# Grouped column products and a reordered hand-over in a two-block transformer kernel on one core

## The reference, cut to what matters

```
compress(kv): 15 blocks of 32 tokens at stride 16, per key/value head
    hid = gelu(flat(block + pos) @ w1)        # 2048 x 256, once for keys, once for values
    out = hid @ w2
hgrn2_chunk_scan(q, k, logf, v), forwards and backwards, 8 heads of width 128
    scores = sum_k q[t,k] * k[s,k] * exp(b[t,k] - b[s,k]),  s <= t
x = x + mixer(rmsnorm(x))
peer_ffn(rmsnorm(x)): queries = xn @ w_q (1024 x 2048); similarities with sub-keys; top-k;
    dense product of xn with all 16384 expert rows; gates; sum with the expert values
```

## Time and profile before

| | |
|---|---|
| median of 3 runs | 1554.14 us |
| profiled execution, its own time | 1552.54 us |
| its span, first to last instruction | 1550.7 us |
| mean granted PE clock | 0.998 |
| PE busy | 1517.3 us in 9966 records |
| POOL busy | 1188.1 us |
| data moved | 268.44 MB, 173 GB/s |

### The profile page before, as it was taken

One profiled execution on the slowest core, in us unless ns is written; L12 is line 12 of the kernel. 1 busy time (PEld: TensorE's weight loads), 2 busy tenths in 40 slices (PEclk: granted clock), 3 DMA queues, 4 the chain that ended last, 5 costly groups with the idle time before them and its releaser, 6 DMA issues.

```text
span 1550.7 us, 28007 instructions
## 1 busy us (share of the span) xinstructions
PE 1517.3 (98%) x9966; PEld 1324.3 (85%) x9966; DVE 946.3 (61%) x1389; ACT 804.1 (52%) x1087; POOL 1188.1 (77%) x499
## 2 busy tenths in 40 slices
PE   7999999999999999999999999999999999999998
PEld 5688888887899989998899998888887777788886
DVE  5545565555432558732159950887888999954444
ACT  4456555557655565454454455555554444444443
POOL 6644698885897955567878998777777777789995
PEclk9999999999999999999999999999999999999999
DMA  7533565554554543345645555555554555566653
GB/s 290 171 123 135 165 203 190 184 187 161 188 188 154 169 132 106 110 162 179 220 153 185 179 182 182 177 169 171 174 169 160 173 171 168 175 221 197 190 192 120
DMA packets 72852, 268.44 MB, mean 173 GB/s; under 512 B 8176, under 2 KB 8448, under 8 KB 71760
## 3 DMA queue, kind: packets, MB, share of 16 engines
q1 hardware_dynamic: 70272, 253.99, 50.4%
q0 software_dynamic: 1648, 7.71, 1.4%
q10 hardware_dynamic: 864, 5.77, 1.0%
HBM read 264.29 MB, written 3.15 MB: 172 GB/s over the span
## 4 chain that ended last, share of the span: by engine, by line
PE 67%; POOL 15%; issue 11%; DVE 2%; DMA 2%; ACT 2%; POOLq 0%; DVEq 0%; SPq 0%; ACTq 0%
PE ps L1211 66%; POOL ring_lo L1281 15%; DMA ring<-in_stream 2%; DVE big L961 1%; ACT ring_hi L1716 0%; DMA big<-in_filt 0%; PE ps L1496 0%; ACT h_both L1729 0%; PE ps L1354 0%; DVE big L974 0%; DVE onehots_j_odd L1147 0%; DVE onehots_i L1139 0%; DVE big L1996 0%; PE ps L1451 0%; DVE h_both L1987 0%
## 5 line engine op out<-in xcount | busy, mean ns | idle before, releaser
L1281 POOL TENSOR_TENSOR ring_lo<-ring,ring_hi 128x1024 fp32r<-128x1024 f32 x472 | 1166.4, 2487 | 338.9 <-ACT ring_hi L1716 336.7
L1211 PE MATMUL ps<-h_both,ring_hi 128*128 128x256 f32 (+1 forms) x2944 | 744.8, 331 | 3.8 <-DVE h_both L1987 2.2
L1716 ACT CAST ring_hi<-ring 128x1024 fp32r<-128x1024 f32 x472 | 491.6, 1051 | 439.3 <-DMA ring<-in_stream 436.5
L1211 PE MATMUL ps<-h_both,ring_lo 128*128 128x256 f32 x2080 | 584.0, 281 | 0.0
L1211 PEld LDWEIGHTS ps<-h_both,ring_hi 128*128 128x128 f32 x2944 | 498.0, 190 | 59.6 <-issue 4.0
L1211 PE MATMUL ps<-ring_hi,h_both 128*128 128x512 f32 (+1 forms) x1408 | 430.6, 383 | 9.7 <-POOL ring_lo L1281 4.6
L1211 PEld LDWEIGHTS ps<-h_both,ring_lo 128*128 128x128 f32 x2080 | 395.3, 190 | 0.3
L1211 PEld LDWEIGHTS ps<-ring_hi,h_both 128*128 128x128 f32 x1408 | 260.8, 189 | 65.8 <-issue 10.5
L1211 PE MATMUL ps<-ring_lo,h_both 128*128 128x512 f32 (+1 forms) x704 | 266.2, 378 | 0.0
L1970 DVE TENSOR_TENSOR h_both<-big,h_both 128x512 fp32r<-128x512 f32 x64 | 134.0, 2095 | 101.4 <-ACT h_both L1729 101.3
L1211 PEld LDWEIGHTS ps<-ring_lo,h_both 128*128 128x128 f32 x704 | 133.2, 189 | 23.0
(11 more groups left out here) (305 smaller groups left out, 1346.7 us busy)
## 6 DMA issues: line engine op xcount, KB each, us to landing
ring<-in_stream SPq DMA_DIRECT2D x480, 512.0 KB, 3.8
residual<-big ACTq DMA_DIRECT2D x2, 1024.0 KB, 4.0
big<-residual ACTq DMA_DIRECT2D x2, 1024.0 KB, 6.6
x<-in_x SPq DMA_DIRECT2D x2, 512.0 KB, 5.6
big<-in_fdecay POOLq DMA_DIRECT2D x1, 1024.0 KB, 8.5
big<-in_w POOLq DMA_DIRECT2D x1, 1024.0 KB, 14.3
wrow<-in_post POOLq DMA_DIRECT2D x2, 512.0 KB, 5.0
big<-in_x ACTq DMA_DIRECT2D x1, 1024.0 KB, 5.0
```

The costliest lines, as they stand in the source:

```text
L1211: return nc.tensor.matmul(out, lhsT, rhs, start=start, stop=stop, skip_group_check=True)
L1281: P.tensor_tensor(ring_lo[:, h % RING, :], ring[:, h % RING, :], ring_hi[:, h % RING, :].bitcast(fp32), ALU.subtract).then_inc(S["split_lo ...
L1716: A.copy(ring_hi[:, h % RING, :], ring[:, h % RING, :]).then_inc(S["split_hi"], 1)
```

## The change

- Compression: the four products of one half go to four column groups of 32 (rows 32b of the bank), `BLK` is padded to 32 columns; the four partial sums are added by a product with a 0/1 table `T_GROUP`, which also transposes; GELU moves behind it. The value weights no longer go through the ring: POOL loads them (2 x 1 MB) into `cmp_values`, and the stream has 476 halves. `cmps_loaded` now counts three loads.
- Levels: for j = 0..7 each step does 16 products of 64 keys by 64 queries, in two column groups, into one bank (four banks in turn); the mask is 64 wide and one copy of 512 columns selects; `spread_near` puts the result in place after step 14 and 15; level m = 64 is copied by ACT.
- The copy of `SMALL_TOTALS` moves behind step 1.
- Mixer output: transposed without the norm's roots, half of it between the sixth and the last two quarters of `out_product`; query products start on half of the contraction; the roots scale the similarities, and a product spreads them over partitions for the operand of the experts (`SCALED`).
- Turns: in slot 63 the second half's first two steps come before the first half's last four; one split moves behind `round_activations(0)`, and `rest(0)` comes before `onehots(33)`.

```diff
@@ compression
-        BLK = area(SCR + 1024, 2, 16, 30)
+        BLK = area(SCR + 960, 2, 16, 32)
+        cmp_values = area(12336, 2, HALF), area(18480, 2, HALF)
...
             pool.dma_start(cmps[:, :], dram["cmps"]).then_inc(S["cmps_loaded"], 16)
+            for n in range(2):
+                pool.dma_start(cmp_values[n].rearrange("p a b -> p (a b)"), dram["cmp_values"][n]).then_inc(S["cmps_loaded"], 16)
...
-                w = weights(W_CMP + 2 * kv + bh // 2, bh % 2)
+                w = (cmp_values[bh // 2][:, bh % 2, :],) if kv else weights(W_CMP + bh // 2, bh % 2)
                 for b in range(4):
-                    last = product(ps[0:30, 2 + kv, 0:256], parts((BLK,), ALL, kv, bh * 4 + b, ALL),
-                                   parts(w, ALL, slice(b * 256, (b + 1) * 256)), bh + b == 0, bh == 3 and b == 3)
+                    last = product(ps[b * 32:b * 32 + 32, 2 + kv, 0:256], parts((BLK,), ALL, kv, bh * 4 + b, ALL),
+                                   parts(w, ALL, slice(b * 256, (b + 1) * 256)), bh == 0, bh == 3)
...
-                    last = nc.tensor.transpose(ps[:, 6 + kv, half * 30:half * 30 + 30], HTOK[0:30, kv, half * 128:(half + 1) * 128],
-                                               ident[0:30, 0:30])
+                    last = mm(ps[:, 6 + kv, half * 30:half * 30 + 30], HTOK[:, kv, half * 128:(half + 1) * 128],
+                              aux[:, T_GROUP:T_GROUP + 30])
...
-            dve.wait_ge(S["cmps_loaded"], 16)
+            dve.wait_ge(S["cmps_loaded"], 48)
@@ levels
+                        for g in range(2):
+                            near = slice(st * 128 + 64 * g, st * 128 + 64 * g + 64)
...
+                            place = (st * 4 + h) * 64
+                            last = mm(ps[64 * g:64 * g + 64, level_bank(n), place:place + 64], keys, queries)
...
-                mask = levels[:, 7 - j, :].bitcast(u32).unsqueeze(1).broadcast_to([128, 4, 128])
-                for st in range(2):
-                    last = V.copy_predicated(AT[hg][:, 3 * st], mask,
-                                             ps[:, 4 + 2 * hg + st, :].rearrange("p (h c) -> p h c", h=4))
+                mask = levels[:, j - 1, :].bitcast(u32).unsqueeze(1).broadcast_to([128, 8, 64])
+                V.copy_predicated(NEAR[hg].rearrange("p s h c -> p (s h) c"), mask,
+                                  by_place(level_bank(n)).rearrange("p s h c -> p (s h) c")).then_inc(S["level_dve"], 1)
...
-            act.wait_ge(S["totals_ready"], 1)
-            A.copy(COPIED_TOTALS, SMALL_TOTALS).then_inc(S["totals_copied"], 1)
             ahead(2 * W_V + 9)
...
+                if n == 1:
+                    act.wait_ge(S["totals_ready"], 1)
+                    A.copy(COPIED_TOTALS, SMALL_TOTALS).then_inc(S["totals_copied"], 1)
@@ mixer output to queries
-            out_product(W_OUT2, merged_parts, lambda quarter: wait_operand("merged", quarter + 1))
-            norm_transposes(3)
-            for s in range(8):
...
+            out_product(W_OUT2, merged_parts, lambda quarter: wait_operand("merged", quarter + 1), lambda: mixer_transposes(0))
+            first_query_slot(0, 0)
+            mixer_transposes(1)
+            first_query_slot(1, 0)
+            first_query_slot(0, 1)
+            first_query_slot(1, 1)
+            for s in range(1, 8):
...
+                wide_product(W_Q + s, s, both=q_both)
+                if s == 1:
+                    pe.wait_ge(S["rstd_ready"], 8)
+                    for t in range(TOK):
+                        last = mm(SPREAD[:, tile(t)], stat[:, ST_RSTD + t:ST_RSTD + t + 1].broadcast_to([128, 128]), ident[:, :])
+                    last.then_inc(S["scale_spread"], 1)
@@ turn to the value table
-            for j in range(2):
+            for j, steps in ((0, range(0, 4)), (1, range(0, 2)), (0, range(4, 8)), (1, range(2, 8))):
...
-            for h in (2 * (W_PEER + 65), 2 * (W_PEER + 65) + 1):
-                split(h)
+            split(2 * (W_PEER + 65))
...
             round_activations(0)
+            split(2 * (W_PEER + 65) + 1)
...
+            rest(0)
             onehots(33)
-            rest(0)
             rest(1)
```

More of the change, by code:

```diff
@@ L236, in halves, with level_bank, by_place @@
         def halves(first, apart, m):
-            return strided(first, (2 * m, 64 // m), (apart + m, 2), (1, m))
+            return strided(first, (2 * m, 32 // m), (apart + m, 2), (1, m))
+        def level_bank(n):
+            return 4 + 2 * (n % 2) + n // 2 % 2
+        def by_place(bank):
+            return ps[:, bank, :].rearrange("p (s h c) -> p s h c", s=2, h=4)
         def whole_totals(m):
@@ L783, in act_second @@
+            ahead(2 * W_Q + 1)
+            query_operands(0)
+            mixer_squares(0)
+            ahead(2 * W_Q + 3)
+            query_operands(1)
+            mixer_squares(1)
+            act.dma_start(dram["residual"], RES).then_inc(S["x_stored"], 16)
             for s in range(8):
                 ahead(2 * (W_Q + s) + 5)
+                if s == 0:
+                    for t in range(TOK):
+                        root("inv_ready", t, 7 + t, "rstd_ready")
+                if s == 4:
+                    for half in range(2):
+                        act.wait_ge(S["tokens_scaled"], half + 1)
+                        c = slice(4 * half, 4 * half + 4)
+                        round_to(h_hi[:, c, :], SCALED[:, c, :])
@@ L1269, in _ @@
                     sp.dma_start(ring[:, r, :], dram["stream"][turn * (RING // 2) + r // 2, :, half(r)]).then_inc(arrived[r], 16)
+            for r in range(2 * NSLOT - turns * RING):
+                sp.wait_ge(S["half_multiplied"], turns * RING + (r + 1 - RING))
+                sp.dma_start(ring[:, r, :], dram["stream"][turns * (RING // 2) + r // 2, :, half(r)]).then_inc(arrived[r], 16)
             for n in range(2 * TOK):
@@ L1608, in _, with out_product @@
             mix_transposes((0, 1), 4)
-            def out_product(n, src, ready):
+            def out_product(n, src, ready, between=None):
                 def quarter_product(nh, kq, w, t):
@@ L2303, in shape_constants @@
     zt[:, 256:] = -tt.reshape(2, 128).T
-    lv = np.zeros((128, 8, 128))
-    for n, m in enumerate((64, 32, 16, 8, 4, 2, 1)):
-        same = (r[:, None] // (2 * m)) == (r[None, :] // (2 * m))
-        lv[:, n] = same & ((r[:, None] // m) != (r[None, :] // m))
-    lv[:, 7] = np.eye(128)
+    lv = np.zeros((128, 6, 64))
+    key, query = r[:, None] % 64, r[None, :64]
+    for n in range(6):
+        lv[:, n] = (key >> (n + 1) == query >> (n + 1)) & (key >> n != query >> n)
     iota = np.tile(np.arange(128), (128, 1))
```

221 lines of the change are left out of this document (153 added, 68 removed).

## The result

The changed kernel takes **1527.34 us** (median of 5 runs, 1525.6 to 1528.02); the kernel before takes 1554.14 (5 runs, 1549.91 to 1555.25). The ratio is 0.9829, 95% interval 0.9816 to 0.9843: 1.7% faster. Two later comparisons of the same two kernels gave 0.9809 (0.9791 to 0.9827) and 0.9811 (0.9795 to 0.9827). The forecast was 1528. The profiled execution took 1527.34 us with a span of 1525.4, 25.3 us less than the span before.

A forecast was written before the change was run, and what follows sets the result against it. PE's own work was taken to bound the kernel nearly everywhere. Gains of 9.1, 9.8, 1.2, 4.2 and 1.4 sum to 25.7 us, taking the profiled 1552.54 to 1526.8; forecast median 1528, own range 1523 to 1533, wider range 1520 to 1538.

The forecast's parts named there:

- compression: Compression products: four overlapping column groups turn 14.16 us into 3.5; net gain 9.1 us.
- levels: The 16 level steps: 64 x 64 records at 33 ns, 18.6 us for 30.1, less added waits; net 9.8 us.
- totals: First channel product: PE's 1.2 us wait for POOL goes once the small totals' copy moves.
- mixer output: Mixer output to end of query slot 0: 7.5 us instead of 12.13, less 0.45 for spreading roots; net 4.2 us.
- turn: Turn between half-tables: PE's 2.01 us wait for the first activations' rest shrinks to 0.6; net 1.4 us.
- The wait for POOL: Ahead of retention_part(0, 0), behind compression: PE arrives before POOL's two rests are done and waits 0.9 us.
- Levels, the waits: At steps 8 and 12, PE's waits for DVE's chain grow to 1.8 and about 1.0; 1.7 us given back.
- rival 3: Levels: DVE becomes the bound, its growths all 4.55 us beside denser POOL work, about 4 us lost; 1532, chance 0.12.
- 1: Levels: records of a 64-column step don't overlap, about 56 ns each, nothing gained there; 1538 us, chance 0.11.
- 2: Levels: fixed serial cost of 50 ns a record, gain 2.9 instead of 9.8 us; 1535 us, chance 0.05.
- 5: Levels: each 64 x 64 record costs 0.11 us like a 128 x 128, 28 us more than now; 1566, chance 0.03.
- 4: Compression: value weights land late, PE's transposes of heads wait about 4.7 us; 1533 us, chance 0.06.

The follow-up runs named there:

- experiment 9: The kernel before, unedited, profiled and timed once more: 1555.0 us, ratio 0.9999 to the other runs of the same kernel.
- experiment 6: Changed kernel with its 32 compression products in one column group again, value weights still beside the ring: 1536.64 us, ratio 0.9888 to the kernel before.
- experiment 2: Changed kernel with grouped records reordered, in the levels all 16 of one column group before the other's: 1533.66 us, ratio 0.9887 to the kernel before.
- experiment 1: Changed kernel with the small totals' copy ahead of the split again, and both turn splits ahead of the first rounding: 1528.46 us, ratio 0.9863.
- experiment 3: Changed kernel with the first mixer transposes behind the whole output product and onehots(33) ahead of the first rest: 1525.26 us, ratio 0.9828.
- experiment 5: Changed kernel with mixer transposes behind the whole product and waiting for the norm's roots; squares, roots and inverses moved earlier: 1530.89 us, ratio 0.9851.
- experiment 10: Changed kernel with ScalarE doing splits, then key join, then activation at n = 6 and 8 only: 1524.89 us, ratio 0.9806 to the kernel before.
- experiment 4: Changed kernel with the key join ahead of the channel product's activation everywhere in the levels: 1533.15 us, ratio 0.988 to the kernel before.
- (8): Changed kernel with the key join ahead of the channel product's activation at n = 6 and 8 only: 1528.54 us, ratio 0.9836.

## Why the prediction came out right

By landmarks of PE that both traces have, in order of time:

| term | predicted | measured | from |
|---|---|---|---|
| compression | 9.1 | 9.5 | the same pause starts at 142.20 before, 132.73 after |
| levels | 9.8 | 11.1 | step 0 to the product behind step 15: 81.46 before, 69.11 after, less the 1.22 below |
| totals | 1.2 | 1.2 | wait gone |
| mixer output | 4.2 | 4.0 | 21.71 ahead at that product, 25.74 at the similarity products |
| turn | 1.4 | 1.8 | 2.01 less 0.25 |
| sum | 25.7 | 27.6 | |
| the rest | 0 | -2.3 | gate stretch -3.1, slots ahead of it -0.5, behind the turn +1.4 (0.8 of it single waits), between compression and levels -0.1 |

The mechanisms were those that the prediction gave; the close agreement of the sum is partly luck, since terms 1.9 us too small met 2.3 us that no term had. The terms of the mixer output and the turn also depend on which profile of the kernel before they start from: by that of experiment 9 they would be 1.4 and 1.3 us larger.

- **Compression.** The group overlap was priced right to 0.4 us (3.86 for 3.5), and experiment 6 shows that it is all of the gain. The wait for POOL was 0.28 and not 0.9: PE came at 78.18, 0.6 us later than assumed, and POOL was done at 78.3 instead of 78.5. (The prediction's own saving of 10.2 us puts PE at 77.4, not 77.6; the 0.8 us from there are 0.36 of longer groups, 0.65 instead of 0.5 for the sum over groups and 0.28 of waiting for DVE's decay of the retention scores.) PE reached `retention_part(0, 0)` 9.1 us earlier, as forecast; the rest of the 9.5 is the wait of 0.35 us by `probabilities(0)`, which the prediction named as gone and did not add.
- **Levels, the records.** 33 ns was taken, 32 measured at the plain steps; the 16 windows are 17.73 us, and the eight channel products behind them last 5.95 instead of 5.83 us, the switches of shape. Together 18.6 or 18.7, as in the sum. Taking 33 ns was right and partly luck: the row had 15 moving columns, and 64 turned out to cost no more. The 40 ns taken as the upper bound was none, since the earlier trace rows are f16 one-hot products. With one group behind the other (experiment 2) a plain float32 record took 53 ns, and the same view of the kernel before has such records with a full-width stationary, at 121 ns each:

```profile
L1211 PE MATMUL ps<-big 128*128 128x64 f32 x96 | 11.6, 272 | 0.0
```

- **Levels, the waits.** This was the term mis-sized: 1.7 us to be given back (1.6 by its own waits: 1.8 and 1.0 less 0.95 and 0.26), 0.75 measured (1.96 of waits after 1.21). A further 0.4 us of the 11.1 were there before and in no term: 0.16 us each ahead of three waits, the ends of last records that the 30.11 us leave out. The place was half wrong as well, step 10 for step 12. The prediction kept the old lengths of DVE's growths. But these depend on whether POOL is at work beside them: the one ahead of step 8 fell to 2.35 us, the one ahead of step 9 rose to 5.60. The Trainium skill (SBUF — State Buffer, Who interferes with whom) says that a DVE operation with two SBUF inputs and a GpSimd one that reads SBUF lock each other out. The trace agrees: growths with both inputs in SBUF last 2.35 to 5.60 us, those with one in PSUM 2.33 to 2.35 in all eight cases, POOL busy or not. So the cause that rival 3 named was at work in one place. As a whole it was wrong: the six growths with both inputs in SBUF took 19.1 us together, not more than the 20.2 before.
- **Totals and turn.** Right in place and cause (experiment 1 for both, experiment 3 for DVE's order at the turn); the turn's remaining 0.25 us is the GELU's.
- **Mixer output.** 7.54 us for 7.5, spreading 0.36 for 0.45. Experiments 3 and 5 show both halves at work, 2.4 us for the place of the transposes and 4.75 more once the roots are waited for. The half clock of the kernel before held from 735.2 to 738.6, longer than the 2.0 us that the prediction read; its sum took the whole 12.13 us and did not need that length.
- **Rivals.** 1, 2 and 5 are ruled out by 32 ns a record at the full clock, 4 by value weights that land 8 us early. The Trainium skill's 60 cycles a matmul (TensorEngine Tiling (Array Packing), Instruction Overhead), an estimate of 25 ns at 2.4 GHz, would have made 12.8 us of the records; 17.7 were measured, and with one group behind the other (experiment 2) 53 ns each. Its advice against taking the tiling from an already small dimension, if 64 counts as one, would have kept one from this step, which gained 11.1 us.

**What stays open.** What sets the pace of the gate stretch. Thirteen profiled executions had 6.113 us a slot five times and 6.213 eight times (one of these with two slots at 6.113 first). The same program had both; it isn't the change. That a wait moves PE from one to the other is seen once (experiment 10) and was not tested. How often the unprofiled runs had the one or the other is not known, so part of the scatter of the medians may be this. Open as well is what makes the clock fall behind a wait: it did behind 1.95 us in experiment 3 and 1.75 in experiment 9, and did not behind 2.16 in experiment 1 and 2.01 in the kernel before, all at the turn.

## What to carry to other kernels

Plain float32 products with few columns gain most by column groups if the groups alternate: 32 ns a record against 53 when 16 of one group follow each other. A wait that one engine's order causes can have a second cause right behind it; at the turn both moves together gained 1.8 us, and taking back either one alone lost 1.9 us or, with the slow clock behind the wait, 3.3. Before you move a call in an engine's list, read what it starts with: the splits inside `take`, not its activation, were what PE needed. And judge such a move by the whole stretch: in experiment 10 two waits shrank and the stretch stayed as long as it was.

## What the runs showed of the hardware

- The wide product runs at two paces at the granted clock 1.00: 6.113 or 6.213 us a slot of 16 pairs of records (512 and 256 moving columns) and 16 one-hot records, so 6 ns a pair between them (in the trace the one-hot records take 0.48 us in both, the pairs 5.63 or 5.74). Each held without a change over 20 slots and more.
- Behind a wait of PE the granted clock fell to 0.50 in some places and not in others, and the length of the wait alone does not tell which: it fell with two waits of 2.22 and 2.13 us (experiment 5) and behind single ones of 3.33 and 2.28 (experiment 4), 2.26 (8), 1.95 (3) and 1.75 (9); it stayed at 1.00 behind 2.16 and 1.92 (experiment 1), 2.01 (the kernel before, at the turn) and 1.32 (3). The same program had both at one place (the kernel before and experiment 9). It cost 1.6 us behind the wait of 1.95 and about 1.4 behind that of 2.26.
- DVE's growths and POOL's rests slow each other: 2.35 against 5.60 us for two growths, 4.7 against 6.30 us for two rests. Growths with one input in PSUM stayed at 2.33 to 2.35 us beside POOL.
- Four records of one column group in a row cost nothing beside alternating ones (four groups of 32, 256 moving columns: 1.02 against 1.00 us); with 16 in a row (two groups of 64, 64 moving columns) a record took 53 ns instead of 32.
